# A weight ring's loads issued on free slots alone, without the wait for an earlier landing

## The chip, the cores and the metric

The kernel runs on one core of one Trainium2 chip. The metric is the device time of one execution in microseconds (us). The engines that matter here are TensorE (PE in the profile, PEld for its weight loads), VectorE (DVE), ScalarE (ACT), GpSimd (POOL) and SyncE (SP; "SPq" is its instruction queue). SyncE computes nothing: it waits on semaphores and issues transfers, which the core's 16 DMA engines carry out.

## The reference

One hybrid decoder block on 512 tokens of width 1024, in float32. After an attention-like part (a projection, a gated DeltaNet, a causal pooling, an output projection) comes a mixture of experts, which takes most of the time:

```python
logits = (xt @ w_router + b_router)
top_val, top_idx = lax.top_k(logits, 4)            # 4 of 32 experts for each token
gates = jax.nn.softmax(top_val, axis=-1)
# for each expert e and each block of tokens that chose it:
gu = xb @ w_gate_up[e] + b_gate_up[e]              # 1024 x 2048
gate = jnp.minimum(gu[:, :1024], 7.0)
up = jnp.clip(gu[:, 1024:], -7.0, 7.0)
act = (up + 1.0) * gate * jax.nn.sigmoid(1.702 * gate)
yb = (act @ w_down[e] + b_down[e]) * gate_weight   # 1024 x 1024
# the rows yb are summed per token, then x = x + sum, then a final RMSNorm
```

All 32 experts are used, so all of `w_gate_up` and `w_down` (12 MB for each expert, 384 MB in all) has to come from memory once.

## The kernel before, in words

Up to about 300 us the kernel does the first part and the routing. From then on it goes through the experts in an order of its own, with 32 token slots to a block; an expert has as many blocks as its tokens need. TensorE runs the loop over blocks: gate and up (line 1986), the gather of the next block's tokens (L1938), the down projection (L2040). VectorE and ScalarE form the activation; ScalarE scales the block's result (L883), and GpSimd scatters it to the buffer `pair_rows` in memory by an indirect transfer (L623). GpSimd issues a scatter only when the one before has landed (L619 to L623), and ScalarE writes the next result into the same buffer `ys` after that.

The weights lie in a ring of `RING` = 20 slots of 1 MB ("units"). An expert has `NU` = 12 units: 8 of `w_gate_up`, then 4 of `w_down`. Unit `n` (counted over all experts) goes to slot `n % 20`. An expert's blocks all use the same 12 slots, and a unit's slot comes free when the expert's last block has used it: TensorE raises `w_used` by one for each unit and block, and a table `tab` tells SyncE the count at which the last block begins (`used`). So 12 slots are held by the expert at work, and 8 lie ahead of it.

The first 20 units are loaded by hand-placed calls. All others are issued by `refill(e)` on SyncE (L460 to L477), strictly in order. From unit 32 to unit 371 they go in pairs: one transfer of 2 MB, from `doubled(n)`; the others are single units of 1 MB. `arrival(n)` gives the semaphore and count that say unit `n` has landed. SyncE is in order too: while it waits at one unit, nothing behind it is issued. After the last refill it waits until all scatters to `pair_rows` but the last expert's have landed, loads `pair_rows` back in four transfers of 2 MB (L486), waits until the last block is done, then for the last scatters, reloads `x1_rows` (L492) and stores the output. Blocks of the last expert are scattered with an add into `x1_rows`.

Of the kernel before, what the change touches and what calls it, by code (L numbers as in the profile page):

```python
# [45 lines left out]
NGU = KD  # L46
NU = KD + KD // 2
RING = 20
AHEAD = 4
EARLY = 2  # L50
LAG = 4

# [1 line left out]
def moe_block(nc, x, attn_norm_w, w_in, conv_w, a_log, dt_bias, dn_norm_w, pool_w, pool_scale, w_out,  # L54
# [3 lines left out]
    with ctx:  # L58
# [269 lines left out]
        def doubled(n):  # L328

            return RING + NU <= n < NU * (E - 1) and n % 2 == 0  # L330

        def arrival(n):

            lead = n - 1 if n % 2 and doubled(n - 1) else n
            loads = [k for k in range(lead % RING, lead + 1, RING) if not (k % 2 and doubled(k - 1))]
            return slot_in[lead % RING], 16 * len(loads)
# [38 lines left out]
        def _(sp):  # L375
# [20 lines left out]
            def load_unit(e, u, slot, units=1):  # L396
                sp.dma_start(unit_dst(slot, units), unit_src(e, u, units)).then_inc(slot_in[slot], 16)
# [62 lines left out]
            def refill(e):  # L460


                used = sp.value_load(tab[0:1, e + USED:e + USED + 1], min_val=0, max_val=MAXB * NU)
                following = {ne: sp.value_load(tab[0:1, VISIT + e + ne:VISIT + e + ne + 1], min_val=0, max_val=E - 1)
                             for ne in (1, 2) if e + ne < E}
                for u in range(NU):
                    n = NU * e + u + RING
                    if n >= NU * E or n % 2 and doubled(n - 1):
                        continue

                    units = 2 if doubled(n) else 1
                    signal, count = arrival(n - AHEAD)
                    sp.wait_ge(w_used, used + (u + units))
                    if e == 0 and u >= NGU:
                        sp.wait_ge(side_ps, 2 + u + 1 - NGU)
                    sp.wait_ge(signal, count)
                    load_unit(following[n // NU - e], n % NU, n % RING, units)  # L477

            for e in range(E - 1):
                refill(e)  # L480
# [1653 lines left out]
```

## Time and profile before

| what | us |
|---|---|
| median of 3 runs | 1334.08 (1334.01 to 1335.76) |
| the profiled execution | 1327.91 |
| its span, first to last instruction | 1325.8 |
| TensorE busy in it | 1268.7 |
| VectorE, ScalarE, GpSimd busy | 585.3, 239.0, 162.7 |
| mean granted TensorE clock | 0.985 |

The span is 2.1 us shorter than the profiled execution's own time, and that time is 6.2 us below the median. Lines such as "L476" are lines of the kernel; a line of a helper stands for all its callers (L397 is the helper `load_unit`, which issues every weight transfer). A transfer is written "out<-in"; its time in the chain of work runs from the end of its issue to its landing. A "share" of DMA is the mean busy share of the 16 DMA engines.

### The profile page before, as it was taken

How to read it: one execution, taken by the hardware profiler on the slowest of the kernel's cores; microseconds unless marked ns; L12 is line 12 of the kernel's file. 1: busy time of each engine (PE TensorE's matmuls, PEld its weight loads, DVE VectorE, ACT ScalarE, POOL GpSimd, SP SyncE). 2: the span in 40 equal slices, each digit the busy share in tenths (PEclk: the TensorE clock that was granted, in tenths of full speed). 3: DMA queues.
4: the chain of work that ended last, by engine and by line, in shares of the span. 5: the costliest groups of instructions: out<-in, count | busy, mean ns of one | idle time of the engine just before them, and what ended most of it. 6: DMA issues, size and time to landing. Idle time of an engine off the chain costs nothing.

```text
span 1325.8 us, 52244 instructions
## 1 busy us (share of the span) xinstructions
PE 1268.7 (96%) x21476; PEld 785.9 (59%) x21477; DVE 585.3 (44%) x2029; ACT 239.0 (18%) x587; POOL 162.7 (12%) x267
## 2 busy tenths in 40 slices
PE   8999999999999999999999999999999999998885
PEld 4545655545666666666566656667656665654552
DVE  5553223447244444444344444444434444443337
ACT  3421123332111111111111111111111111111112
POOL 4100420122110110101101101011010110100011
PEclk9999999999999999999999999999999999999998
DMA  7453131629899999999999999999999999999997
GB/s 239 140 185 120 33 141 50 256 76 379 355 423 396 420 412 419 401 412 391 422 386 421 411 396 398 422 410 416 398 393 411 406 416 375 417 428 414 421 424 315
DMA packets 56019, 455.68 MB, mean 344 GB/s; under 512 B 8338, under 2 KB 20299, under 8 KB 28011
## 3 DMA queue, kind: packets, MB, share of 16 engines
q1 hardware_dynamic: 51920, 445.68, 82.8%
q0 software_dynamic: 3888, 8.40, 1.7%
q8 instruction: 87, 1.43, 0.4%
q14 instruction: 18, 0.14, 0.0%
q10 hardware_dynamic: 106, 0.04, 0.0%
HBM read 432.53 MB, written 23.27 MB: 344 GB/s over the span
## 4 chain that ended last, share of the span: by engine, by line
DMA 50%; PE 46%; DVE 2%; issue 1%; SPq 0%; POOL 0%; ACT 0%; POOLq 0%; DVEq 0%; ACTq 0%
DMA ring<-in_w_gate_up_dram 29%; DMA ring<-in_w_down_dram 19%; PE ps L1986 14%; PE ps L1540 11%; PE ps L2040 7%; PE ps L1560 4%; PE ps L1938 2%; PE ps L1601 2%; DMA x_rows_dram<-cat,rowi 1%; PE ps L1594 1%; PE ps L2020 1%; PE ps L1502 0%; DMA ring<-x_rows_dram 0%; DVE ring L1493 0%; PE ps L1686 0%
## 5 line engine op out<-in xcount | busy, mean ns | idle before, releaser
L1986 PE MATMUL ps<-ring,cat 128*32 128x256 f32 x9856 | 555.5, 382 | 4.5 <-DMA ring<-in_w_gate_up_dram 4.3
L1986 PEld LDWEIGHTS ps<-ring,cat 128*32 128x32 f32 x9856 | 342.2, 111 | 197.8 <-issue 10.2
L2040 PE MATMUL ps<-ring,cat 128*32 128x256 f32 x4800 | 283.9, 386 | 29.7 <-DMA ring<-in_w_down_dram 27.3
L2040 PEld LDWEIGHTS ps<-ring,cat 128*32 128x32 f32 x4800 | 145.6, 111 | 137.0 <-issue 38.6
L1540 PE MATMUL ps<-hbuf,ring 128*128 128x512 f32 x320 | 147.7, 607 | 1.7 <-DVE hbuf L958 1.7
L1349 DVE TENSOR_REDUCE wslot<-ps 128x2 f32<-128x6 f32 x75 | 12.3, 164 | 301.7 <-ACT cat L883 300.2
L856 ACT ACTIVATE cat<-cat 128x128 f32<-128x128 f32 x154 | 47.8, 310 | 492.1 <-DVE cat L1384 471.7
L623 POOL DMA_INDIRECT pair_rows_dram<-cat,rowi x73 | 72.8, 997 | 424.1 <-ACT cat L883 424.1
L1938 PE MATMUL ps<-hbuf,cat 128*32 128x256 bf16 x2432 | 111.5, 275 | 0.0
L1379 DVE TENSOR_TENSOR cat<-ps,cat 128x128 f32<-128x128 f32 x148 | 57.2, 387 | 98.5 <-PE ps L1986 87.8
L1540 PEld LDWEIGHTS ps<-hbuf,ring 128*128 128x128 f32 x320 | 58.8, 191 | 68.3 <-issue 66.7
L883 ACT ACTIVATE cat<-ps,wslot 128x256 f32<-128x256 f32 x75 | 35.6, 474 | 346.7 <-PE ps L2040 340.6
L1938 PE MATMUL ps<-aux,cat 128*32 128x256 bf16 x1216 | 96.3, 275 | 0.0
L1938 PEld LDWEIGHTS ps<-hbuf,cat 128*32 128x32 bf16 x2432 | 75.7, 95 | 13.9 <-DVE cat L1458 0.4
L619 POOL TENSOR_TENSOR rowi<-rowj,qcol 128x1 int32<-128x1 int32 x75 | 15.4, 205 | 444.7 <-DMA pair_rows_dram<-cat,rowi 428.3
L1453 DVE COPY selu<-E 96x32 bf16 x75 | 13.4, 178 | 125.3 <-issue 125.3
L1560 PE MATMUL ps<-ring,cat 128*128 128x512 f32 x128 | 58.6, 600 | 0.9 <-issue 0.9
L869 ACT ACTIVATE cat<-ps 128x256 f32<-128x256 f32 x148 | 55.6, 376 | 17.8 <-PE ps L1986 12.5
L1458 DVE TENSOR_TENSOR cat<-iotaf,rank 128x512 bf16 x75 | 51.9, 692 | 12.0 <-DVE gie L1454 12.0
L1381 DVE TENSOR_TENSOR cat<-ps,cat 128x128 f32<-128x128 f32 x148 | 56.5, 382 | 0.0
L1393 DVE STREAM_TRANSPOSE cat<-cat 128x128 f32<-128x128 f32 x154 | 48.0, 312 | 5.3
L1392 DVE TENSOR_TENSOR cat<-cat 128x128 f32<-128x128 f32 x154 | 45.2, 294 | 5.2
(376 smaller groups left out, 911.0 us busy)
## 6 DMA issues: line engine op xcount, KB each, us to landing
ring<-in_w_gate_up_dram SPq DMA_DIRECT2D x112, 2048.0 KB, 10.2
ring<-in_w_down_dram SPq DMA_DIRECT2D x58, 2048.0 KB, 9.5
ring<-in_w_gate_up_dram SPq DMA_DIRECT2D x32, 1024.0 KB, 9.6
ring<-in_w_down_dram SPq DMA_DIRECT2D x12, 1024.0 KB, 10.1
ring<-in_w_in_dram SPq DMA_DIRECT2D x10, 1024.0 KB, 6.4
pair_rows_dram<-cat SPq DMA_DIRECT2D x4, 2048.0 KB, 11.0
ring<-pair_rows_dram SPq DMA_DIRECT2D x4, 2048.0 KB, 20.7
ring<-in_w_out_dram SPq DMA_DIRECT2D x1, 4096.0 KB, 12.8
```

The lines of the kernel that those rows point to most:

```text
L623: G.indirect_dma_start(out=into, out_offset=bass.IndirectOffsetOnAxis(ap=rowi[:, 0:1], axis=0), in_=ys, in_offset=None, bounds_check=limit ...
L856: A(sg[:, half], gc[:, half], ACT.Sigmoid, scale=ALPHA).then_inc(sg_ok, 1)
L869: A(biased[half], ps[:, BIAS, 2 * P * half:2 * P * (half + 1)], ACT.Copy).then_inc(bias_copied, 1)
L1379: V.tensor_tensor(chunked_half(gc[:, half]), in_order(ps[:, b, 0:P]), in_order(bias[half][:, 0:P]), ALU.add).then_inc(uc_step, 1)
L1381: V.tensor_tensor(chunked_half(uc[:, half]), in_order(ps[:, b, P:2 * P]), in_order(bias[half][:, P:2 * P]), ALU.add).then_inc(uc_step, 1)
L1393: V.transpose(to[:, half], act_[:, half]).then_inc(told, by)
L1458: step(V.tensor_tensor(hot[:, :, :, :], slots, mine, ALU.is_equal), hot_ok, count)
L1540: last = mm(bank(m % 2), win[:, piece % 3, k, m % 2 * P:(m % 2 + 1) * P], hT[:, k, :], start=k == 0, stop=k == KD - 1)
L1560: last = mm(bank(n % 2), catT[:, k, b * P:(b + 1) * P], wout[:, k, 512 * half:512 * (half + 1)], start=i == 0, stop=i == KD - 1)
L1938: last = mm(ps[SLOTS * q:SLOTS * (q + 1), 2, 0:QD].rearrange("p (m c i) -> p m c i", c=2, i=SLOTS), hot[:, b, 0, :], rows, start=b == 0 an ...
L1986: last = mm(ps[SLOTS * q:SLOTS * (q + 1), banks[half], 0:2 * P].rearrange("p (s r) -> p s r", s=2), x[:, SLOTS * u:SLOTS * (u + 1)], quart ...
L2040: last = mm(ps[SLOTS * q:SLOTS * (q + 1), 1, 0:QD], actT[:, c // 4, SLOTS * (c % 4):SLOTS * (c % 4 + 1)], w[:, i, q * QD:(q + 1) * QD], st ...
```

## The change

SyncE no longer waits until the unit four places ahead in the queue (so, with pairs, the transfer two places ahead) has landed. What is left is the wait that the slots are free. Order, sizes, slots and all other engines' code stay.

```diff
 RING = 20
-AHEAD = 4
 EARLY = 2
...
                     units = 2 if doubled(n) else 1
-                    signal, count = arrival(n - AHEAD)
                     sp.wait_ge(w_used, used + (u + units))
                     if e == 0 and u >= NGU:
                         sp.wait_ge(side_ps, 2 + u + 1 - NGU)
-                    sp.wait_ge(signal, count)
                     load_unit(following[n // NU - e], n % NU, n % RING, units)
```

In the compiled program the landing wait (traced at L476) stands ahead of the wait for `w_used` (traced as a register operation at L397).

## Rows read from the trace of the kernel before

**Rows 1.** The page: the span, and the DMA share in 40 equal slices of it.

```profile
span 1325.8 us, 52244 instructions
...
DMA  7453131629899999999999999999999999999997
```

**Rows 2.** The chain that ended last, shares of the span by engine.

```profile
DMA 50%; PE 46%; DVE 2%; issue 1%; SPq 0%; POOL 0%; ACT 0%; POOLq 0%; DVEq 0%; ACTq 0%
```

**Rows 3.** The same chain in time, 548 to 575 us: start, us, what.

```profile
551.46 10.86 DMA ring<-in_w_down_dram
...
562.33 0.02 SPq L476
...
562.52 10.27 DMA ring<-in_w_gate_up_dram
```

**Rows 4.** Waits of SyncE, 350 to 1287 us: total us, times, longest us.

```profile
SPq L476 <- DMA ring<-in_w_gate_up_dram: 433.3, 119, 5.8
SPq L476 <- DMA ring<-in_w_down_dram: 278.1, 58, 6.5
SPq L397 <- PE ps L1986: 50.0, 18, 9.4
```

**Rows 5.** Stretches: length, busy of five engines, granted clock, DMA share, GB/s.

```profile
350.00:370.00 20.00, 17.92 (x328) 10.54 (x320) 8.04 (x32) 2.93 (x9) 1.17 (x2) 0.91 0.79 314
674.00:681.00 7.00, 7.00 (x152) 4.23 (x148) 4.05 (x17) 0.88 (x3) 1.17 (x2) 1.00 0.71 255
681.00:736.00 55.00, 54.89 (x1125) 35.56 (x1120) 24.18 (x97) 8.18 (x23) 4.69 (x8) 1.00 1.01 424
742.00:801.00 59.00, 56.43 (x1140) 35.93 (x1132) 24.34 (x96) 7.86 (x23) 4.96 (x9) 0.97 1.00 406
801.00:808.00 7.00, 7.00 (x152) 4.21 (x148) 4.05 (x17) 0.91 (x3) 1.17 (x2) 1.00 0.79 283
991.00:998.00 7.00, 7.00 (x156) 4.24 (x152) 4.05 (x18) 0.82 (x3) 1.17 (x2) 1.00 0.79 279
1119.00:1125.00 6.00, 6.00 (x132) 3.58 (x124) 3.36 (x12) 0.58 (x2) 1.07 (x2) 1.00 0.71 240
...
1280.00:1305.00 25.00, 17.98 (x372) 10.82 (x364) 14.80 (x37) 4.02 (x9) 4.05 (x5) 0.97 1.02 421
350.00:1287.00 937.00, 903.34 (x18136) 579.82 (x18124) 403.66 (x1592) 126.86 (x362) 85.83 (x146) 0.99 0.99 407
```

**Rows 6.** Waits of TensorE for weights, whole run.

```profile
PE ps L2040 <- DMA ring<-in_w_down_dram: 27.3, 16, 3.7
```

**Rows 7.** DMA issues: count, KB each, median us from issue to landing.

```profile
ring<-in_w_gate_up_dram SPq DMA_DIRECT2D x112, 2048.0 KB, 10.2
...
ring<-pair_rows_dram SPq DMA_DIRECT2D x4, 2048.0 KB, 20.7
...
pair_rows_dram<-cat,rowi POOLq DMA_INDIRECT x73, 6.8
```

**Rows 8.** `pair_rows_dram`: all scatters; then landings of one in 800:804, one in 580:585.

```profile
L623 POOL DMA_INDIRECT pair_rows_dram<-cat,rowi x73: 993/994/1212, 334.7 to 1272.5; - x73
...
DMA to landing us min/median/max: 3.4/3.4/3.4
...
DMA to landing us min/median/max: 7.8/7.8/7.8
```

**Rows 9.** Waits of GpSimd, 330 to 1262 us.

```profile
POOL pair_rows_dram L623 <- ACT cat L883: 418.6, 72, 11.7
```

**Rows 10.** The chain at the end: the last two scatters.

```profile
1289.94 11.19 DMA x_rows_dram<-cat,rowi
...
1304.17 5.51 DMA x_rows_dram<-cat,rowi
```

**Rows 11.** SyncE in order of time, 1262 to 1285 us: start, us, transfers.

```profile
1269.81 7.98 SPq L397 DMA_DIRECT2D ring<-in_w_down_dram  x4
1279.41 1.76 SPq L486 DMA_DIRECT2D ring<-pair_rows_dram  x4
```

## The prediction, made before the change was run

> **What bounds the kernel now.** I read the slices first: from the tenth on, the DMA engines are at nine tenths or more to the end [rows 1]. Then the chain that ended last: half of it is DMA and 46% TensorE [rows 2], so the expert stage passes between a transfer bound and a TensorE bound. Followed in time, the DMA parts have one shape: a transfer lands, SyncE's landing wait (L476) ends within 0.02 us, the next pair is issued 0.2 us later, and that pair takes 10.3 to 10.9 us to land [rows 3]. SyncE's waits agree: between 350 and 1287 us it stood 711.4 us in 177 landing waits and only 50.0 us in 18 waits for free slots [rows 4].
>
> A hasty reader would conclude that the landing wait paces the stream. It doesn't, and the reader should see why. A pair has a median of 10.2 us from issue to landing [rows 7]. It is 2 MB (2048 KB, 2.097 million bytes), which at 424 GB/s [rows 5] takes 4.95 us, and two of them 9.9 us. The wait lets two pairs be in flight, and the 10.2 us of each are its own 4.95 behind the 4.95 of the pair ahead plus some 0.3 of start and end. When it opens, one whole pair still lies ahead of the engines, 4.95 us of work, and the issue needs 0.2 us. The stretches say the same: 681:736 holds a dozen such waits, at a DMA share of 1.01 and 424 GB/s [rows 5]. The share reads 1.01 to 1.02 when nothing is idle, so I take 1.01 as full.
>
> Where are the engines not full? In 350:370, 674:681, 801:808, 991:998 and 1119:1125 the share is 0.79, 0.71, 0.79, 0.79 and 0.71 [rows 5]. These stretches hold SyncE's waits for slots (18 of them, up to 9.4 us, for TensorE's L1986 [rows 4]): an expert with many blocks holds its 12 slots until its last block, and the stream runs dry. TensorE is busy in them (7.00 of 7.00 us and the like): there it is the bound.
>
> **The change part by part.**
>
> *The wait instruction itself.* 177 of them go between 350 and 1287 us [rows 4], each some 0.02 us once satisfied [rows 3], while a pair ahead covers SyncE's 0.2 us. On the path: 0. If that cover were gone (the stream dry), the new transfer would be 0.02 us earlier, 18 times: 0.4 us at most.
>
> *Idle time that the wait makes on the DMA engines.* This is the only time that it can give back. The stretch 350:1287 has a mean share of 0.99 [rows 5]; against 1.01 that is 0.02 x 937 = 18.7 us idle. The five dry stretches hold 0.22 x 20 + 0.30 x 7 + 0.22 x 7 + 0.22 x 7 + 0.30 x 6 = 4.4 + 2.1 + 1.5 + 1.5 + 1.8 = 11.3 us of it. The rest, 7.4 us, is shared by the shorter of the 18 slot waits and by the landing wait (an engine that is a pair ahead of the slowest one has nothing to do until that one lands). So the gain is between 0 and 7.4 us. It is nearer to 0: 681:736, full of landing waits, shows none at all, and a transfer lands when its slowest engine is through, which by then already has the next pair's share queued and was never idle. Only where the slowest engine changes from one transfer to another is something won. I take 0.8 us, and keep 0 and 7.4.
>
> *What is moved earlier.* SyncE will issue a pair as soon as its slots are free. In 177 - 18 = 159 cases they were free when the landing wait opened, so in most of the stage more transfers will be in flight. At most 8 slots lie ahead of an expert with blocks to come, and up to 12 more come free in its last block; with TensorE waiting for what has just landed, four to six pairs can be queued. Landings stay where they were, since the queue is served in order and was full: the issue moves, the bytes do not. The median from issue to landing should grow from 10.2 to 20 to 30 us and mean nothing.
>
> *Behind SyncE's wait.* The table reads at the start of each refill and the end sequence are what else is queued. The reload of `pair_rows` at 1279.41 [rows 11] waits for the last scatter to `pair_rows`, issued at 1272.5 [rows 8] with the median of 6.8 us to land [rows 7], so until 1279.3: not for the weight loads ahead of it. It stays, and at 1.02 the engines are full there anyhow [rows 5].
>
> *Does a deep queue cost bandwidth?* The trace has one place with a deep queue: single units issued 1269.81 to 1277.8 are followed by four reloads of 2 MB from 1279.41 [rows 11], so that around 1281 some 10 to 11 MB are in flight instead of 4. In 1280:1305 the engines moved 421 GB/s at 1.02 [rows 5], against 424 with two pairs in flight. The difference of 0.7% would be 0.007 x 937 = 6.6 us slower if it held everywhere; but other stretches with two pairs in flight move only 406 [rows 5], so 421 is well within what depth two gives. I take 0.
>
> *Does a deep queue delay the scatters?* They are GpSimd's, on another queue of the same engines. The one issued in 800:804, beside a dry stream, landed in 3.4 us, the one in 580:585, beside a full stream, in 7.8 [rows 8]; the median is 6.8 [rows 7]. So a full stream adds some 3.5 to 4.4 us. It does not add the whole queue: with two pairs ahead that would be up to 9.9 us. GpSimd then still waits 418.6 / 72 = 5.8 us each time for ScalarE [rows 9], so a scatter may take 5.8 us longer than now before anything waits for it. I take 0 for it.
>
> The Trainium skill, page "DMA: Bandwidth & Descriptors", section "Queues, rings and completion order", speaks against this last point in one rule: the descriptor that raises a transfer's semaphore lands only after every earlier write of that DMA engine, across its queues. By it a scatter's landing is tied to weight writes that the engine has begun. The two landings of 3.4 and 7.8 us agree with some such tie. The same section says that an engine takes turns between its queues packet by packet; by that, weight transfers still waiting in SyncE's queue don't count and the term stays 0. No row here has ordinary scatters beside four or more pairs.
>
> **Sum.** 0 - 0.8 + 0 + 0 + 0 = 0.8 us off the profiled execution's 1327.91, so 1327.1. The median of the runs shown is 6.2 us above that execution; I carry the difference over: 1334.08 - 0.8 = 1333.3 us.
>
> **The rivals.**
>
> *R1, no change beyond the forecast (likeliest): 1333.3, with an own range of 1331.5 to 1336.* TensorE's path can't gain either: it waits 27.3 us for `w_down` in 16 places [rows 6], and those waits end with landings that don't move. That depth never rises, because slots are the tighter limit, is ruled out by the 159 cases; it would end in the same time.
>
> *R2, slower: a deeper queue makes the packets slower.* With all engines free to run far ahead of each other, memory could be read less well. For: at the same share, stretches differ from 424 to 406 GB/s [rows 5], so something other than idling costs up to 4%, and I can't name it. Against: the 421 at the deep place [rows 5]. If the stage ran 1% slower, it would cost 0.01 x 937 = 9.4 us: 1343. It decides from 0.3% (2.8 us). Chance 0.18.
>
> *R3, slower: the scatters become the pace.* From a landing to the next issue GpSimd and ScalarE need 1304.17 - (1289.94 + 11.19) = 3.04 us [rows 10]. Scatters follow one another in (1272.5 - 334.7) / 72 = 13.0 us [rows 8]. So from a landing time of 13.0 - 3.0 = 10.0 us on they set the pace. With four reloads queued a scatter (the adding kind) took 11.19 us, with little queued 5.51 [rows 10]. If ordinary ones took 11.2, a block would take 1.2 us more: 72 x 1.2 = 86 us, 1420. This is the way in which the skill's rule on the semaphore, quoted above, would hurt. Chance 0.07.
>
> *R4, faster: the 7.4 us are mostly the landing wait's.* If at least half are and the slowest engine changes often, 3.7 to 7.4 us are won: 1330.4 to 1326.7. Against it stands 681:736 with no idle time. A higher rate (424 where there is now 406) would end there too. Chance 0.13.
>
> **How the numbers follow.** Chances: R1 0.62, R2 0.18, R3 0.07, R4 0.13. The time is R1's. A change of under 0.2% (2.7 us) can't be told from none here. Faster by more is R4: 0.13; slower by more is R2 and R3: 0.25; the rest 0.62. The range takes in R1, the near end of R4 and R2 up to 0.6%: 1330.3 to 1342. That leaves out about 0.06 below, and R3 and the upper part of R2, 0.12, above.
>
> **What would show it.** In the profile after: the L476 waits gone; SyncE's slot waits up from 50 to several hundred us, in nearly every issue; median issue to landing of the pairs 20 us or more; mean DMA share over the stage 0.99 as before and GB/s within 1 of 407; the dry stretches at the same experts with the same length; scatters still at 6.8 us median, GpSimd's wait for ScalarE near 5.8 us each; TensorE's wait for `w_down` near 27 us. Wrong: a rate below 405 at a share of 1.00 or more (R2); scatters at 10 us or more with GpSimd's wait gone (R3); a rate above 409 (R4).

## The result, and the profile after

The change made the kernel faster: 1312.52 us median (1310.7 to 1315.09) against 1334.05 us (1331.66 to 1335.76, with a fourth run), a ratio of 0.984 with a 95% interval of 0.982 to 0.986. That is some 21 us, where 0.8 was forecast and 3.8 at most was allowed for by the range. The profiled execution of the changed kernel took 1315.09 us, the slowest of its four, and that of the kernel before 1327.91, less than any of the four runs behind its median, so the two traces differ by only 12.8 us. What they show is the mechanism; the size is the ratio's.

The page of the changed kernel, its span, and the chain by engine:

```profile
span 1313.1 us, 52055 instructions
...
DMA  7453131619999999999999999999999999999996
...
PE 73%; DMA 22%; DVE 2%; issue 1%; POOL 0%; DVEq 0%; ACT 0%; SPq 0%; POOLq 0%; ACTq 0%
```

The DMA slices look as in [rows 1]. The chain turned over, from half DMA [rows 2] to 73% TensorE. Part of that is only how a chain is followed: before, it went from each landing through SyncE's landing wait to the next; now no instruction waits there. SyncE's waits, 350 to 1272 us:

```profile
SPq L396 <- PE ps L1983: 625.5, 115, 27.2
SPq L396 <- PE ps L2037: 114.5, 58, 3.0
SPq L483 <- DMA pair_rows_dram<-cat,rowi: 13.8, 1, 13.8
```

The landing waits are gone and the slot waits grew from 50 to 740 us (the lines moved up by three: L396 is L397 of before, L1983 is L1986, L2037 is L2040). Issues, with the median us from issue to landing:

```profile
ring<-in_w_gate_up_dram SPq DMA_DIRECT2D x112, 2048.0 KB, 24.9
ring<-in_w_down_dram SPq DMA_DIRECT2D x58, 2048.0 KB, 13.8
...
pair_rows_dram<-cat,rowi POOLq DMA_INDIRECT x73, 7.1
```

The `w_gate_up` pairs wait 24.9 us instead of 10.2 [rows 7], in a queue that is now deep; the scatters moved from 6.8 to 7.1. So far nearly all is as forecast (only the `w_down` pairs, at 13.8, stay short of the 20 us or more). The stretches are not:

```profile
350.00:370.00 20.00, 17.87 (x327) 10.50 (x325) 7.74 (x30) 2.44 (x7) 1.17 (x2) 0.91 0.77 305
350.00:1272.00 922.00, 899.04 (x18151) 580.44 (x18148) 403.88 (x1592) 126.89 (x362) 85.32 (x146) 0.99 0.99 415
...
1120.00:1272.00 152.00, 135.68 (x2652) 84.86 (x2644) 59.22 (x234) 18.43 (x53) 12.44 (x23) 0.97 1.01 426
```

The expert stage moved 415 GB/s where it had moved 407, and at the same mean DMA share of 0.99 [rows 5]. The reader should stop at this: more bytes at an equal busy share. The first dry stretch, 350:370, is as before. The stage's 937 x 407 GB/s would take 919 us at 415, 18 less; in the chain the last `w_down` unit landed at 1272.50 us instead of 1287.45 (below, and [rows 10] for the scatter that follows it), 15 earlier. The end after it took 2 us longer. First the line of the kernel before, then those of the changed one:

```profile
1277.46 9.99 DMA ring<-in_w_down_dram
```

```profile
1249.56 22.94 DMA ring<-in_w_down_dram
...
1275.00 10.82 DMA x_rows_dram<-cat,rowi
...
1287.97 6.57 DMA x_rows_dram<-cat,rowi
...
1295.41 7.57 DMA ring<-x_rows_dram
```

TensorE's waits for weights fell, for `w_down` from 27.3 [rows 6] to 11.7:

```profile
PE ps L2037 <- DMA ring<-in_w_down_dram: 11.7, 13, 1.5
PE ps L1983 <- DMA ring<-in_w_gate_up_dram: 8.8, 4, 3.7
```

**Where the bandwidth came from.** The share counts a DMA engine as busy from a packet's start to its end. A pair is cut into packets of 16 KB, eight for each engine, and nearly all take 0.611 us; 16 engines x 16384 bytes / 0.611 us is 429 GB/s, which is also the highest rate in the 40 slices of the changed kernel's page. These are the stretches 370 to 1260 us of both kernels, the one before first:

```profile
370.00:1260.00 890.00, 862.09 (x17352) 554.84 (x17346) 384.75 (x1520) 121.28 (x346) 81.84 (x138) 0.99 0.99 409
```

```profile
370.00:1260.00 890.00, 872.62 (x17664) 565.09 (x17660) 391.71 (x1547) 123.55 (x352) 83.50 (x141) 0.99 0.99 417
```

In them I counted the 16 KB packets of the weights that took over 0.73 us (1.2 times 0.611), the time beyond 0.611 in them ("excess"), and the time in which an engine had no packet at all ("idle"), from the packet records (times are means over the 16 engines):

```
                         GB/s   long packets   excess in them   idle
kernel before           408.6            918          26.3 us   14.3 us
changed kernel          417.1            308          10.6 us   11.7 us
```

The excess fell by 15.7 us and the idle time by 2.6, together 18.3 us. The rate alone says the same: 890 x (1 - 408.6 / 417.1) = 18 us. Six sevenths of that was time that the profile calls busy.

What a long packet is can be seen where the stream had run dry. In the kernel before SyncE issued a pair at 676.99 us:

```profile
676.99 2.06 SPq L397 DMA_DIRECT2D ring<-in_w_down_dram  x2
```

After it the records have, as start and length in us:

```
677.98 1.02   678.00 0.70   678.02 1.02   678.03 1.44   678.03 1.40   678.03 1.78
678.08 1.19   678.20 0.94   678.20 2.03   678.21 1.46   ...   679.74 0.61   679.76 0.61
```

The first packets begin 1.0 us after the start of the issue (which itself takes 0.33 us; the times of transfers in the chain run from its start too, not from its end) and take up to 2 us instead of 0.61. So after an empty queue the recorded time of a packet holds something beyond the moving of its bytes. I read it as the wait for the first bytes; the records don't say what it is. In the kernel before the long ones stand in the middle of full stretches too. When each engine's packets are strung together by their times (16 engines aren't labelled, so this is approximate), between 370 and 1180 us 262 long packets directly follow the small semaphore write that ends a transfer; in the changed kernel 10 do. I take those for engines that had finished a transfer and had nothing queued. They are the first packets only: they hold some 9 of the 25 us of excess in that stretch, and about as much lies in packets further on in the same transfers, which fell from 8 to 2 us in the changed kernel. The rest follows packets of scatters and instruction loads, and stayed at 8 us.

### The profile page after: what moved, and what is told of

Read it like the earlier page. It is cut to its first block, busy times and chain, and to the rows that moved or that the text cites. A ratio compares the mean times of both kernels' runs of the same rounds, so it can differ in the third digit from the quotient of the medians.

```text
span 1313.1 us, 52055 instructions
## 1 busy us (share of the span) xinstructions
PE 1263.9 (96%) x21477; PEld 785.1 (60%) x21477; DVE 586.7 (45%) x2029; ACT 239.2 (18%) x587; POOL 161.0 (12%) x267
## 4 chain that ended last, share of the span: by engine, by line
PE 73%; DMA 22%; DVE 2%; issue 1%; POOL 0%; DVEq 0%; ACT 0%; SPq 0%; POOLq 0%; ACTq 0%
PE ps L1983 30%; DMA ring<-in_w_down_dram 19%; PE ps L2037 15%; PE ps L1537 11%; PE ps L1935 5%; PE ps L1557 4%; PE ps L1598 2%; DMA x_rows_dram<-cat,rowi 1%; PE ps L2028 1%; PE ps L1944 1%; PE ps L1591 1%; DMA ring<-x_rows_dram 1%; DMA pair_rows_dram<-cat,rowi 1%; PE ps L1499 0%; DMA pair_rows_dram<-cat,sm 0%
## 5 line engine op out<-in xcount | busy, mean ns | idle before, releaser
L1983 PE MATMUL ps<-ring,cat 128*32 128x256 f32 x9856 | 555.7, 382 | 9.0 <-DMA ring<-in_w_gate_up_dram 8.8
L1983 PEld LDWEIGHTS ps<-ring,cat 128*32 128x32 f32 x9856 | 343.5, 111 | 199.2 <-DMA ring<-in_w_gate_up_dram 10.7
L2037 PE MATMUL ps<-ring,cat 128*32 128x256 f32 x4800 | 277.9, 380 | 14.5 <-DMA ring<-in_w_down_dram 11.7
L2037 PEld LDWEIGHTS ps<-ring,cat 128*32 128x32 f32 x4800 | 144.4, 110 | 119.4 <-issue 19.7
L1386 DVE SCALAR_TENSOR_TENSOR cat<-cat 128x128 f32<-128x128 f32 x154 | 45.6, 296 | 5.3
## 6 DMA issues: line engine op xcount, KB each, us to landing
ring<-in_w_gate_up_dram SPq DMA_DIRECT2D x112, 2048.0 KB, 24.9
ring<-in_w_down_dram SPq DMA_DIRECT2D x58, 2048.0 KB, 13.8
```

The lines of the kernel that those rows point to most:

```text
L1983: last = mm(ps[SLOTS * q:SLOTS * (q + 1), banks[half], 0:2 * P].rearrange("p (s r) -> p s r", s=2), x[:, SLOTS * u:SLOTS * (u + 1)], quart ...
L2037: last = mm(ps[SLOTS * q:SLOTS * (q + 1), 1, 0:QD], actT[:, c // 4, SLOTS * (c % 4):SLOTS * (c % 4 + 1)], w[:, i, q * QD:(q + 1) * QD], st ...
```

## The experiments

Theory A: with the landing wait, engines that are ahead of the slowest one run dry before the next pair reaches them, and show it as long packets. What counts is the **margin**, the work that lies ahead of the slowest engine when the wait opens, against the engines' lead plus the way from issue to first bytes. Theory B: what counts is the **depth**, the number of bytes in flight. Theory C: what counts is that SyncE can issue in bursts.

### e1 and e6: the wait kept, six places ahead

```diff
-AHEAD = 4
+AHEAD = 6
```

> The landing wait is kept, but on the unit six places ahead instead of four, so three pairs (6 MB) may be in flight instead of two. Theory A (engines that run ahead of the slowest one find their queue empty, because the next pair is issued only when the slowest engine has landed the pair before last; part of that starving is counted as busy, as packets that take longer than 0.611 us): one more pair of 4.9 us ahead is more than the spread of the engines, so nearly the whole gain comes back: ratio to the kernel before 0.982 to 0.988, 407 GB/s rises to about 415 in the expert stage. Theory B (the depth itself: the more transfers are queued, the faster the memory is read): 6 MB is one step of three or four, ratio 0.993 to 0.997. Theory C (what counts is that SyncE is free to issue in a burst when an expert's slots come free): three pairs in flight still hold the bursts back, ratio 0.995 to 1.000.

Measured: ratio 0.991 (0.989 to 0.993), 1315.56 us median. That is between the ranges of A and B. One of its four runs took 4572.61 us, which the ratio leaves out, and its profile showed the rate of the changed kernel, 417 GB/s in 370:1260, and 301 long packets. So it was run again, beside the changed kernel on the same chip:

> The landing wait six places ahead once more, with five rounds, since the first measurement (0.9909) held one disturbed run and its profile showed no more lengthened packets than the changed kernel. Theory A: within 0.4% of the changed kernel. A remainder theory (a second part of the gain that needs four or more transfers queued): 0.5% or more behind it.

Measured: 0.986 (0.982 to 0.990), 1311.85 us, 316 long packets. The changed kernel itself, for which the expectation was:

> The changed kernel itself, on the same chip as the runs beside it, to rank it against the wait with six ahead. All theories: ratio 0.981 to 0.987.

came to 0.986 (0.982 to 0.990), 1312.45 us. The two can't be told apart, so the remainder theory falls. SyncE still stood in landing waits in most cases; this is e1, 370 to 1260 us:

```profile
SPq L476 <- DMA ring<-in_w_gate_up_dram: 347.7, 94, 6.0
SPq L476 <- DMA ring<-in_w_down_dram: 257.4, 57, 6.3
SPq L397 <- PE ps L1986: 117.5, 46, 8.6
```

and this the kernel before in the same window:

```profile
SPq L476 <- DMA ring<-in_w_gate_up_dram: 420.6, 111, 5.8
SPq L476 <- DMA ring<-in_w_down_dram: 272.4, 57, 6.5
```

605 us of landing waits instead of 693, three pairs in flight at most, and the whole gain. Theory C falls, and the wait as such costs nothing.

### e2: eight places ahead

The same line with `AHEAD = 8`.

> The landing wait on the unit eight places ahead: four pairs (8 MB) may be in flight. Theory A: same as with six ahead within 0.2%, ratio 0.981 to 0.988. Theory B: a further clear step beyond six ahead, 0.3 to 0.5% faster than that one. Theory C: between six ahead and no wait, 0.990 to 0.995.

Measured: 0.986 (0.984 to 0.988), 1309.27 us; 417 GB/s and 313 long packets. Against e1, on the same chip, that is a step of some 0.4%, as B has it; against the repeat e6, with six runs and a ratio of the same 0.986, it is none. The traces side with e6: 417 GB/s in e1, e6 and e2, with 301, 316 and 313 long packets. But e1's trace is of its fastest run, 1311.08 us, so what its two slower ones (1314.12 and 1316.99 us) lost stays open.

### e3 and e4: single units, the same depth with more margin

```diff
 def doubled(n):
-    return RING + NU <= n < NU * (E - 1) and n % 2 == 0
+    return False
```

With the wait four places ahead (e3), 4 MB may be in flight as before, but it opens at each unit, with three of them, 7.3 us of work, ahead. e4 is the control, without the wait.

> All refills as single units of 1 MB, with the kernel before's landing wait on the unit four places ahead. As much is in flight as before (4 MB), but when the wait opens three units (7.3 us of work) lie ahead instead of one pair (4.9 us). Theory A: the engines that are ahead by 2 to 3 us no longer run dry, so most of the gain appears at the same depth: 0.5 to 1.5% faster than the kernel before once the price of smaller packets is taken off, which the run without the wait shows; packets of 8 KB take 0.309 us, 1.1% more per byte, so ratio 0.990 to 1.003, and the same as single units without the wait within 0.4%. Theory B: no gain at 4 MB: ratio 1.005 to 1.015, and at least 1% slower than single units without the wait.

> All refills as single units of 1 MB, without any landing wait: the control for the run with single units and the wait. Theories A and B alike: the gain of the change less the price of 8 KB packets: ratio 0.985 to 0.998. Theory A has it within 0.4% of single units with the wait; theory B at least 1% faster than those.

Measured: e3 0.987 (0.984 to 0.989), 1311.38 us; e4 0.985 (0.984 to 0.987), 1308.17 us. e3 is better than expected, and e4 at the good end of its range: the price of small packets was made up by slots that come free one by one, so that the dry stretches nearly vanish (idle 2.0 us in 370:1260 instead of 11.7). Between the two lies 0.2%. The profile of e3, its issues with the median to landing, then a stretch:

```profile
ring<-in_w_gate_up_dram SPq DMA_DIRECT2D x256, 1024.0 KB, 10.0
ring<-in_w_down_dram SPq DMA_DIRECT2D x128, 1024.0 KB, 9.8
```

```profile
370.00:1260.00 890.00, 874.56 (x17728) 556.99 (x17720) 391.74 (x1547) 123.29 (x352) 84.65 (x141) 0.99 1.01 418
```

418 GB/s with 4 MB in flight and 10 us from issue to landing, just as in the kernel before. The 8 KB packets take 0.309 us; 241 of them took over 0.371 us (1.2 times that) in 370:1260 in e3 and 229 in e4, so the wait made next to none. B wanted e3 at 1.005 or more, and e4 at least 1% faster than e3; theory B falls.

### e7: single units, three places ahead

`AHEAD = 3` on top of e3: the kernel before's margin of 4.9 us, with 3 MB in flight.

> Single units with the landing wait three places ahead: 3 MB in flight, and two units (4.9 us) ahead of the engines when the wait opens, the same as the one pair of the kernel before. Theory A: the margin decides, so the loss of the kernel before is back: ratio 0.995 to 1.010, about 1% or more behind single units with four ahead (0.9867). Theory B: 3 MB against 4 MB is one small step in depth: ratio 0.988 to 0.993.

Measured: 0.992 (0.989 to 0.995), 1318.7 us. It is 0.6% behind e3, not the 1% or more that A gave, and its value lies in B's range:

```profile
370.00:1260.00 890.00, 867.31 (x17552) 555.05 (x17547) 389.37 (x1537) 122.44 (x350) 83.21 (x140) 0.99 1.01 412
```

Its rate, 412 GB/s against e3's 418, shows that the loss is back, but only about two thirds of it. By its ratio alone this run doesn't decide. Its packets speak for A: 837 took over 0.371 us, where e3 has 241, with 20.4 us of excess against 6.2.

### e8, e10: the kernel before, with a later issue

Table reads stand between the opening of the landing wait and the issue, three in e8 and one in e10. They compute nothing that is used.

```diff
+                    sp.wait_ge(signal, count)
+                    for _ in range(3):
+                        sp.value_load(tab[0:1, e + USED:e + USED + 1], ...)
                     sp.wait_ge(w_used, used + (u + units))
...
-                    sp.wait_ge(signal, count)
```

> The kernel before with three extra table reads on SyncE between the opening of the landing wait and the issue, 1.7 us for each refill (its own three reads take that long at each expert). Nothing of the computation changes. Theory A: the margin of 4.9 us shrinks to 3.2, below the lead of most engines plus the time from issue to first packet, so every transfer makes them wait: ratio 1.01 to 1.06 and many more lengthened packets, though two transfers may still be in flight. Theory B (depth alone): still two pairs in flight nearly always, ratio 0.999 to 1.005.

> The kernel before with one extra table read between the opening of the landing wait and the issue (0.57 us instead of 1.7). Theory A: the dose counts, and more than in proportion to it, since few engines are beyond the limit now: 0.8 to 2.5% slower than the kernel before, ratio 1.008 to 1.025. Theory B: no change, 0.998 to 1.002.

Measured: e8 1.071 (1.065 to 1.077), 1426.14 us, beyond even A's range, so A had the direction but too small a size; e10 1.022 (1.014 to 1.029), 1363.36 us, within it. So 1.7 us later at each issue costs 95 us in all, and 0.57 us some 30. The stretch of e8:

```profile
350.00:1250.00 900.00, 825.68 (x16186) 514.56 (x16178) 359.08 (x1416) 112.63 (x322) 75.45 (x128) 0.96 0.96 370
```

370 GB/s at a share of 0.96: the share fell by 3% against [rows 5] while the rate fell by 9%. At most two pairs are in flight, as before.

### e9, e11: the same late issue with more margin

e9 is e8 with `AHEAD = 6`; e11 is the changed kernel with the three reads.

> The same three extra table reads before every issue (1.7 us), but with the landing wait six places ahead. Theory A: two pairs (9.8 us of work) lie ahead when the wait opens, so 1.7 us more or less doesn't matter: ratio 0.983 to 0.992, as without the extra reads. If instead SyncE's extra work itself cost the 7% of the run with four ahead, the ratio would stay above 1.05.

> The changed kernel with the three extra table reads before every issue. All theories: SyncE has time, so the reads are hidden: ratio to the kernel before 0.983 to 0.990.

Measured: e9 0.986 (0.980 to 0.992), 1313.68 us; e11 0.986 (0.981 to 0.992), 1311.02 us. The delay that cost 7% costs nothing once a second pair lies ahead. Stretches of e9 and of e11:

```profile
370.00:1260.00 890.00, 870.99 (x17669) 560.99 (x17665) 390.81 (x1544) 123.27 (x352) 83.63 (x141) 0.99 0.99 417
```

```profile
370.00:1260.00 890.00, 867.36 (x17619) 560.57 (x17611) 390.41 (x1541) 122.44 (x350) 82.34 (x140) 1.00 0.99 416
```

### e12: two places ahead, no margin

> The landing wait two places ahead: one pair in flight, and nothing ahead of the engines when it opens. Theory A: each pair then costs its whole way from issue to landing on empty engines, about 7.8 us, plus 0.2 us to issue, so some 8.0 us for 2 MB, 262 GB/s, in place of 5.2: 170 pairs x 2.8 = 480 us more, ratio about 1.35. Theory B has no figure of its own for this; a ratio below 1.15 would speak against A.

Measured: 1.378 (1.369 to 1.388), 1833.78 us. Its chain around 710 us and its stretch:

```profile
702.27 8.10 DMA ring<-in_w_gate_up_dram
...
710.58 7.70 DMA ring<-in_w_down_dram
...
718.49 7.65 DMA ring<-in_w_down_dram
```

```profile
370.00:1260.00 890.00, 651.03 (x11464) 371.14 (x11459) 255.47 (x1008) 79.72 (x228) 53.33 (x91) 0.86 0.72 261
```

A pair on empty engines takes 7.7 to 8.1 us, and 261 GB/s is A's 262 (its ratio of 1.35 was a little low). Even here the share, 0.72 of 1.01, makes the loss look like 29%; it is 39% of 429.

**All pairs together**, 370 to 1260 us, counted as above:

```
kernel                     margin at opening       GB/s   long packets   excess   idle
e12  two ahead             none                   261.1           2151     90.7  255.6
e8   four ahead, +1.7 us   4.9 us, issue at 1.9   369.6           2677     77.5   40.2
e10  four ahead, +0.57     4.9 us, issue at 0.8   389.6           1894     56.9   21.5
before, four ahead         4.9 us, issue at 0.2   408.6            918     26.3   14.3
e9   six ahead, +1.7 us    9.9 us, issue at 1.9   416.9            327     10.8   12.4
e6   six ahead             9.9 us, issue at 0.2   417.0            316     10.7   11.9
e2   eight ahead           14.8 us                417.0            313     10.2   12.3
changed, no wait           slots alone            417.1            308     10.6   11.7
```

The row of e10 is its slowest execution, 1373.88 us where the others took 1350.72 to 1366.34, so its rate is a little low.

The rate depends on the margin left at the issue, and has stopped rising where that is 8 us (e9); no run with pairs lies between 4.7 and 8, and single units are at their full rate with 7.3 us less 0.2. Depth can't make this order: before, e8 and e10 all allow two pairs in flight. A later issue also lowers the mean of what is in flight, so that I worked it out too, as the rate times the mean time from the end of the issue to landing in the semaphore records (9.7, 9.7, 9.3, 9.6 and 7.2 us): before 3.8 MB, e10 3.6, e8 3.3, e3 3.8, e7 2.8. At an equal 3.8 MB, e3 moves 418 GB/s and the kernel before 409; and e7 with the least in flight moves 412, e8 with more only 370. The mean depth doesn't order the rates either. The 300 long packets that remain at any depth are another matter; some two thirds follow packets of the scatters and of instruction loads, and no run went after them.

## Why the prediction was wrong

**The chain and the landing wait.** Right as far as it went: the wait isn't serial with the stream, and a pair's 10.2 us are mostly the pair ahead. The conclusion drawn, that the stream is full, was not.

**"Idle time that the wait makes on the DMA engines. This is the only time that it can give back."** This is the step that failed. It took the busy share for the measure of use, with 7.4 us as the most that could be won. (The shares have two digits, so that its 18.7 us were known only to some 5 us either way; that isn't what failed.) The wait cost some 21 us by the ratio and 18 by the two traces, 15.7 of which were long packets, which the share counts as busy. The check was at hand: 1.01 x 429 GB/s is 433, and 350:1287 moved 407 at 0.99 [rows 5], where the same share of full packets would be 424 (0.99 / 1.01 of 433). That is 4%, 37 us, of which the wait was about half.

**"A transfer lands when its slowest engine is through, which by then already has the next pair's share queued and was never idle. Only where the slowest engine changes from one transfer to another is something won."** The mechanism was named rightly and sized at 0.8 us without a count. The spread was measurable: the semaphore records of the kernel before have a pair's first engine landing on average 2.1 us ahead of its last, in one case out of ten over 2.8, and 3.6 at most. Against it stands 4.9 - 0.2 (issue) - 1.0 (to the first packet) - some 1 (its excess) = 2.7 us, an estimate from the packets after 676.99. The engines' lead was just at the limit, which would also explain why 0.57 us more cost so much. And the wait itself held that lead down: in the changed kernel the first engine lands 2.6 us ahead on average, in one case out of ten over 5.2. That a smaller margin lengthens more packets and slows the whole stream is what e8 to e10 show; that it is the engines with a lead that starve, and when, was only reconstructed.

**"681:736 holds a dozen such waits, at a DMA share of 1.01 and 424 GB/s."** One good stretch was taken for all. It has 26 long packets; 742:801, with the same waits at a share of 1.00, has 105 and moves 406.

**R2's puzzle.** The prediction saw the difference from 424 to 406 at equal share and said "something other than idling costs up to 4%, and I can't name it", then used it as a reason to fear a slowdown. It was the best clue to the gain. R4 mentioned a higher rate and gave it no time of its own.

**The other terms.** The wait instruction itself: 0, right (e1 keeps it at no cost). The queue gets deep, to 24.9 us for `w_gate_up` (13.8 for `w_down`, where 20 or more was forecast): right in kind. Bandwidth of a deep queue: no loss, right. Scatters: 7.1 us against 6.8 and GpSimd still waits 395.5 us in 72 times for ScalarE (418.6 before [rows 9]), so R3 didn't come, and the tie to weight writes that the Trainium skill, page "DMA: Bandwidth & Descriptors", section "Queues, rings and completion order", gives for the semaphore cost 0.3 us at most with the deeper queue. "TensorE's path can't gain": wrong, since landings moved; its `w_down` waits went from 27.3 to 11.7 us. The last point of the list of signs had it: "a rate above 409 (R4)" is what happened, with a chance of 0.13.

**A better version.** None of the runs is clearly ahead of the changed kernel: single units without the wait (0.985) and eight ahead (0.986) overlap with its 0.984 and 0.986.

## What to carry to other kernels

If a transfer is issued when an earlier one has landed, the wait opens with the slowest DMA engine. Ask how much work then lies ahead, and compare it with the spread of the landings plus the time from issue to first bytes; a spread measured under such a wait is held down by it. Here three transfers of 2 MB in flight were enough, and four of 1 MB, where two and three were not. Don't read the busy share as use: divide the bytes moved by what the shortest packets give, and look at the lengths of packets.

## What the runs showed of the hardware

- A packet's recorded time is longer after an empty queue: the first 16 KB packets of the pair issued at 676.99 us took 0.7 to 2.0 us instead of 0.611. The busy share counts this in full.
- The cost of a late issue is steep at the limit: 0.57 us later at each of some 190 issues cost 2.2%, 1.7 us cost 7.1%, and with one pair more ahead neither delay nor depth changed anything (417 GB/s).
- Depth up to the ring's limit did no harm: the median scatter took 4.1 us to land with one pair in flight (e12), 6.8 with two, and 7.1 with `w_gate_up` pairs queued for 25 us.
- The lead of a transfer's first engine over its last grows when no wait holds it: 2.1 us on average in the kernel before, 2.6 in the changed one, with 5.8 at most instead of 3.6.
